# Four score tiles without the split, a first selection round by head, and two splits moved into the gates

## The reference, cut to what matters

```python
def peer_ffn(h, w_q, sub_keys, expert_u, expert_v):      # heads 8, keys 128, top 16
    def block(hb):
        q = (hb @ w_q).reshape(n, PEER_HEADS, 2, PEER_HALF_2)
        s = jnp.einsum('nhcd,hckd->nhck', q, sub_keys).astype(jnp.float32)
        sc, ix = lax.top_k(s, PEER_TOPK)
        cand = sc[:, :, 0, :, None] + sc[:, :, 1, None, :]
        cidx = ix[:, :, 0, :, None] * PEER_N_KEYS + ix[:, :, 1, None, :]
        top, pos = lax.top_k(cand.reshape(n, PEER_HEADS, PEER_TOPK * PEER_TOPK), PEER_TOPK)
        eidx = jnp.take_along_axis(cidx.reshape(n, PEER_HEADS, -1), pos, axis=-1)
        gate = jax.nn.softmax(top, axis=-1)
        act = jax.nn.gelu(jnp.einsum('nhed,nd->nhe', expert_u[eidx], hb), approximate=False)
        return jnp.einsum('nhe,nhed->nd', (gate * act).astype(hb.dtype), expert_v[eidx])
```

## Time and profile before

| what | value |
|---|---|
| median of three runs | 3543.71 us |
| profiled execution, its span | 3543.48 us, 3541.7 us |
| TensorE matmul busy | 3328.0 us, 94% |
| VectorE busy | 2326.8 us, 66% |
| ScalarE busy | 1489.2 us, 42% |
| GpSimd busy | 388.7 us, 11% |
| mean granted TensorE clock | 0.967 |
| load of a tile of `u`, issue to landing, median | 4.2 us |

### The profile page before, as it was taken

How to read it: one execution, slowest core, us unless ns; L and a number is a source line. 1 busy time by engine, 2 the same in 40 slices (tenths; PEclk the granted TensorE clock), 3 DMA queues, 4 the chain that set the end, 5 groups by cost and what they waited for, 6 DMA issues and landing times. The chain is left out here.

```text
span 3541.7 us, 58730 instructions
## 1 busy us (share of the span) xinstructions
PE 3328.0 (94%) x20974; PEld 2901.7 (82%) x20974; DVE 2326.8 (66%) x4418; ACT 1489.2 (42%) x2295; POOL 388.7 (11%) x412
## 2 busy tenths in 40 slices
PE   6889999999988898999999997989788999999998
PEld 5788899999977587899999986578478889999996
DVE  4697666666656588666666665555459766666665
ACT  3336444444445325544444433333333644444444
POOL 0156000000000047200000000000015600000000
PEclk9999999999999699999999998999999999999999
DMA  5420555555544231355555544100242055555553
GB/s 209 154 73 27 187 185 189 189 183 185 189 164 154 84 114 43 125 189 184 185 188 189 184 164 175 63 1 1 95 155 72 31 190 183 185 189 189 184 184 145
DMA packets 127132, 511.72 MB, mean 144 GB/s; under 512 B 14625, under 2 KB 15521, under 8 KB 119713
## 3 DMA queue, kind: packets, MB, share of 16 engines
q1 hardware_dynamic: 127008, 510.09, 40.3%
HBM read 508.99 MB, written 1.05 MB: 144 GB/s over the span
## 5 line engine op out<-in xcount | busy, mean ns | idle before, releaser
L610 PE MATMUL ps<-xh,uhigh 128*128 128x256 f32 x3072 | 870.6, 283 | 0.0
L612 PE MATMUL ps<-xh,ulow 128*128 128x256 f32 x3072 | 869.3, 283 | 0.0
L611 PE MATMUL ps<-xl,uhigh 128*128 128x256 f32 x3072 | 869.2, 283 | 0.0
L610 PEld LDWEIGHTS ps<-xh,uhigh 128*128 128x128 f32 x3072 | 588.3, 192 | 15.0 <-issue 1.4
L611 PEld LDWEIGHTS ps<-xl,uhigh 128*128 128x128 f32 x3072 | 588.3, 192 | 14.3 <-issue 1.4
L612 PEld LDWEIGHTS ps<-xh,ulow 128*128 128x128 f32 x3072 | 588.3, 192 | 0.0
L760 ACT CAST uhigh<-stream 128x1024 fp32r<-128x1024 f32 x336 | 352.8, 1050 | 439.0 <-DMA stream<-in_u 439.0
L992 DVE TENSOR_TENSOR ulow<-stream,uhigh 128x1024 fp32r<-128x1024 f32 x330 | 404.4, 1225 | 192.1 <-ACT uhigh L760 192.1
L997 DVE TENSOR_TENSOR stream<-stream,big 128x256 f32<-128x256 f32 x336 | 218.0, 649 | 413.9 <-ACT stream L822 413.9
L628 PE MATMUL ps<-vhigh,chigh 128*128 128x512 f32 x1536 | 479.7, 394 | 1.5 <-DVE vlow L1008 1.5
L628 PE MATMUL ps<-vlow,chigh 128*128 128x512 f32 x1536 | 475.9, 391 | 0.0
(11 more groups left out here) (502 smaller groups left out, 4387.1 us busy)
## 6 DMA issues: line engine op xcount, KB each, us to landing
stream<-in_u SPq DMA_DIRECT2D x369, 512.0 KB, 4.2
stream<-in_v SPq DMA_DIRECT2D x369, 512.0 KB, 3.5
big<-in_wq SPq DMA_DIRECT2D x24, 1152.0 KB, 7.0
stream<-in_ab_w_in SPq DMA_DIRECT2D x4, 2048.0 KB, 10.9
stream<-in_c_w_qf SPq DMA_DIRECT2D x16, 512.0 KB, 3.5
stream<-in_c_w_ig SPq DMA_DIRECT2D x4, 2048.0 KB, 7.9
big<-in_w_gates SPq DMA_DIRECT2D x4, 2048.0 KB, 7.9
spare<-in_u SPq DMA_DIRECT2D x15, 512.0 KB, 3.7
```

What stands on the lines that cost most here:

```text
L610: pe.matmul(out, high[:, cols], c.xh[:, k, :], start=k == 0, stop=False)
L611: pe.matmul(out, high[:, cols], c.xl[:, k, :], start=False, stop=False)
L612: ins = pe.matmul(out, low[:, cols], c.xh[:, k, :], start=False, stop=k == KD - 1)
```

## The change

Five edits, all in `peer`:

1. The tiles 12 to 15 (`WHOLE` = 12) are no longer split. TensorE multiplies `u` by `xt` as they are, in 8 matmuls for a tile (`whole_scores`), each of which becomes two passes on the engine, as the queries do. Tile 15 comes after the transposes. Banks 2 and 3 hold the results of tiles 14 and 15. No B table may be written before tile 15 is done, so VectorE and GpSimd wait for it.
2. ScalarE's exponentials come before the gelus of tiles 12 to 15, not behind all gelus.
3. The splits of tiles 16 and 17 move into the gates: their rounding before ScalarE's copies 9 and 17, and their subtraction from GpSimd to VectorE, before the weighted rows of quads 20 and 28.
4. The first selection round goes head by head (`halves_by_head`): all of `halves` for a head, then for the other.
5. Two tiles, not four, are scored after the second round of heads, and four after the third.

```diff
-    AFTER = {1: range(0, 4), 2: range(4, 6)}
+    AFTER = {1: range(0, 2), 2: range(2, 6)}
+    WHOLE = 12
...
     def early_bank(n):
-        return c.ps[:, 6 + n % 2, 0:T]
+        return c.ps[:, (6 if n < HELD - 2 else 2) + n % 2, 0:T]
...
             def early(n):
-                sp.wait_ge(low_done, n - 2)
+                if n - 3 < WHOLE:
+                    sp.wait_ge(low_done, n - 2)
+                else:
+                    sp.wait_ge(early_used, n - 2)
...
-            for b in range(2):
-                sp.wait_ge(low_done, HELD - 2 * b)
+            for b in (1, 0):
+                sp.wait_ge(early_used, HELD - 2 * b)
...
+            def whole_scores(n):
+                pe.wait_ge(early_landed[n % 3], 16 * (n // 3))
+                pe.wait_ge(early_gelu, n - 1)
+                for k in range(KD):
+                    ins = pe.matmul(early_bank(n), early_u[n % 3][:, k * P:(k + 1) * P], c.xt[:, k, :],
+                                    start=k == 0, stop=k == KD - 1)
+                ins.then_inc(early_used, 1)
...
-            for n in range(6, HELD):
+            for n in range(6, WHOLE):
                 early_scores(n)
+            for n in range(WHOLE, HELD - 1):
+                whole_scores(n)
...
-            pe.wait_ge(keys_ready, 1)
-            pe.wait_ge(early_gelu, HELD)
-            distances_of(0)
...
+                if x == 0:
+                    pe.wait_ge(early_gelu, HELD - 2)
+                    distances_of(0)
+            whole_scores(HELD - 1)
+            pe.wait_ge(early_gelu, HELD)
...
             act.activation(c.sel[:, 2], c.sel[:, 2], ACT.Exp).then_inc(exp_ready, 1)
+            for n in range(WHOLE, HELD):
+                early_act(n)
...
             for g in range(QUADS):
+                if g in (9, 17):
+                    u_high(0, g // 16, False)
...
+            def halves_by_head():
+
+                for g in range(GROUP):
+                    own = [(tt * GROUP + g) * 2 + half for tt in range(NT) for half in range(2)]
+                    dve.wait_ge(sc_ready, g + 1)
+                    dve.sem_inc(passed, 1)
+                    for q in own:
+                        link.mark(dve.max(TOP[:, q, 0:8], SCq[:, q, :]))
...
-                halves(r)
                 if r:
+                    halves(r)
                     store(r - 1)
+                else:
+                    halves_by_head()
...
-            dve.wait_ge(early_gelu, HELD)
...
+            weighted_rows(0)
+            dve.wait_ge(early_gelu, HELD)
+            plain_rows(0)
...
+                if g in (20, 28):
+                    b = (g - 20) // 8
+                    dve.wait_ge(uh_ready, b + 1)
+                    dve.tensor_tensor(ul[:, b], u[:, b], uh[:, b].bitcast(F32), ALU.subtract).then_inc(u_split, 1)
+                weighted_rows(g)
...
-            for n in range(9, HELD + 2):
+            for n in range(9, WHOLE):
                 early_low(n)
             alone(selt_ready, 1)
+            alone(early_used, HELD)
```

More of the change, by code:

```diff
@@ L757, in u_high @@
                 else:
-                    act.wait_ge(early_used, HELD - 2 * b)
-                    act.wait_ge(low_done, HELD - 2 * b)
+                    act.wait_ge(early_used, WHOLE)
                 act.copy(uh[:, b], u[:, b]).then_inc(uh_ready, 1)
@@ L840, in _ @@
             link = Link(dve, chain)
+            def halves_by_head():
[5 more added lines that the diff above has]
+                        link.mark(dve.max(TOP[:, q, 0:8], SCq[:, q, :]))
+                    link.join_alone(passed)
+                    for q in own:
+                        link.mark(dve.max_index(IDX[:, q, 0:8], TOP[:, q, 0:8], SCq[:, q, :]))
+                        link.mark(dve.match_replace(REST[:, q, :], TOP[:, q, 0:8], SCq[:, q, :], LOWEST))
+                    link.join_alone(passed)
+                    for q in own:
+                        link.mark(dve.max(TOP[:, q, 8:16], REST[:, q, :]))
+                    link.join_alone(passed)
+                    for q in own:
+                        link.mark(dve.max_index(IDX[:, q, 8:16], TOP[:, q, 8:16], REST[:, q, :]))
+                dve.sem_inc(sc_used, 1)
             def halves(r):
@@ L958, in gate_held, with plain_rows @@
                                   ALU.mult).then_inc(dve_moved, 1)
-            for g in range(0, QUADS, 2):
-                if g >= 4:
-                    dve.wait_ge(g_ready, g - 2)
+            def plain_rows(g):
                 for x in (g, g + 1):
@@ L975, in _ @@
                                              bc(c.selt[:, 2, t:t + 4], 2, P), ALU.is_equal, ALU.mult).then_inc(a_ready, 1)
+            weighted_rows(0)
+            dve.wait_ge(early_gelu, HELD)
+            plain_rows(0)
+            for g in range(2, QUADS, 2):
+                if g >= 4:
+                    dve.wait_ge(g_ready, g - 2)
+                plain_rows(g)
+                if g >= 4:
+                    gate_held(g - 4)
+                    gate_held(g - 3)
+                if g in (20, 28):
[3 more added lines that the diff above has]
+                weighted_rows(g)
             for g in range(QUADS - 4, QUADS):
@@ L1021, in early_low @@
             def early_low(n):
-                if n < HELD:
-                    alone(high_done, n + 1)
-                    high, low, raw, done = early_uh[n % 3], early_ul[n % 3], early_u[n % 3], low_done
-                else:
-                    alone(uh_ready, 2)
-                    high, low, raw, done = uh[:, n - HELD], ul[:, n - HELD], u[:, n - HELD], u_split
-                pool.tensor_tensor(low, raw, high.bitcast(F32), ALU.subtract).then_inc(done, 1)
+                alone(high_done, n + 1)
+                pool.tensor_tensor(early_ul[n % 3], early_u[n % 3], early_uh[n % 3].bitcast(F32), ALU.subtract
+                                   ).then_inc(low_done, 1)
             def pick(r):
```

10 lines of the change are left out of this document (2 added, 8 removed).

## The result

| | before | after |
|---|---|---|
| median of the runs, us | 3544.22 (4 runs, 3543.57 to 3545.14) | 3524.47 (4 runs, 3520.92 to 3524.60) |
| profiled execution: time, span, us | 3543.48, 3541.7 | 3524.60, 3522.8 |
| granted TensorE clock over the span | 0.967 | 0.973 |
| copy of quad 3, us from a layer's start, three layers | 132.86, 134.78, 133.34 | 125.22, 125.25, 125.54 |
| copy of quad 3 to the first rounding of `v`, us, three layers | 77.72, 77.71, 77.70 | 79.35, 79.35, 79.35 |

The ratio is 0.9943, with a 95% interval of 0.9931 to 0.9955: 19.8 us faster, against 15.5 forecast (3528.0, range 3516 to 3540). A layer's start is the cast of the activations on ScalarE (L784, before L772); it stands at 130.84, 1227.64 and 2595.76 us after, at 129.40, 1232.10 and 2606.96 before.

What follows compares the result with a forecast made beforehand. VectorE's serial list, stalled by GpSimd's subtractions, was taken to bound the time ahead of the gates, a chain through four engines the gates. 3543.48 - 23.0 (copy of quad 3 earlier) + 7.5 (splits in the gates) = 3528.0 us, range 3516 to 3540.

Steps and rivals of the forecast that it cites:

- The stalls were GpSimd's: Last selection round, cast of keys, product of weights: GpSimd's subtractions hold VectorE; the product ends 8.6, 9.4, 8.6 us earlier.
- the rival in which the long instructions are VectorE's own: Rival, chance 0.04: these VectorE instructions are long whatever GpSimd does, 24.8 us are not won, 3552.8 us, slower.
- Tile 15: Undivided tile between the transposes and the first B tables, 245.4 to 248.9; takes back 4.1 of the first layer's 8.6 us.
- distances and transposes 2.0: TensorE's work just ahead of tile 15, taken as 2.0 us, from at most 2.8 us at 0.78 of the clock.
- about 126 us behind a layer's start in all three layers: Expected place of quad 3's copy in the profile after; its gains were counted as 7.0, 9.0 and 7.0 us.
- The first round by head, two tiles later: nothing: Selection rounds: VectorE's 4.1 us only become waiting for GpSimd's picking; later tiles, zero to 1 us a layer; both counted zero.
- the rival in which round 0 pays: Rival, chance 0.07: the picking and last round come earlier with VectorE, 4.1 us a layer more won, 3515.7 us.
- The splits in the gates: Two ScalarE roundings and two VectorE subtractions in the gates cost 2.5 us a layer, 7.5 in all; bounds nothing to 5.9.
- The idle shares of a mean pair of quads: In the gates, mean idle time, VectorE 0.61 us, ScalarE 0.41; only what a split's instructions exceed it by was counted.
- The rival in which the gates take all back: Rival, chance 0.09: every moved split costs its upper bound, 17.7 rather than 7.5 us in all, 3538.2, no change.
- The port rule: Two-input VectorE and SBUF-reading GpSimd instructions exclude each other; for the gates' subtractions 1.3 us a layer more, 3531.9 us.

## Why the prediction was right, point by point

*The stalls were GpSimd's.* Right. The three small instructions gave back 5.40 us where 5.41 were counted, the cast 1.76 of 1.76, the product 1.41 of 1.42. The product ends 8.7, 9.4 and 8.7 us earlier from the layer's start, for 8.6, 9.4 and 8.6. The subtractions put back brought the stalls back, and only for the instructions that they stood beside. That rules out the rival in which the long instructions are VectorE's own. One reading was loose: the prediction set the ends of L890, L904, L915 and L945 against the rule for two inputs, but L890 (a cast) and L915 (by a scalar) have one. That one-input instructions of this kind are held as well is shown by the fills, which held L945 and L948 of the kernel after.

*Tile 15.* The mechanism was right, the term "distances and transposes 2.0" mis-sized: they took 1.23 us. The prediction named the cause, TensorE busy up to them and at full clock, but priced it from "at most 2.8 us at 0.78 of the clock". That 0.78 is the mean of a window that holds both levels. The narrower window of the kernel before shows the level that the distances and transposes ran at:

```profile
250.00:254.00 4.00, 2.53 (x8) 1.08 (x8) 3.45 (x7) 1.03 (x4) 3.16 (x3) 0.50 0.00 0
```

They took 2.53 us at 0.50, and half of that is 1.27, an estimate that would have been close to the 1.23 measured. Copy 3 so gains 7.64 + 9.53 + 7.79 = 24.96 us rather than 23.0. A small slip adds to this: an event "about 126 us behind a layer's start in all three layers" would gain 7.5 us in the third layer by the prediction's own figures (133.3 - 125.8), and 7.0 were counted. The experiment with the four subtractions shows what the full clock is worth: 2.7 us in the first layer.

*The first round by head, two tiles later: nothing.* Right, both by their own experiment, and for the reason given: L908 behind the picking, and the last round's L917 behind the low part of tile 11. That also excludes the rival in which round 0 pays.

*The splits in the gates.* Right in kind, 7.5 us counted and 3 x 1.64 = 4.9 measured. The copies after fall back by 0.42 us between quads 9 and 12, by 1.0 at quads 20 and 21 and by 0.2 at 28 and 29. The idle shares of a mean pair of quads were too coarse a measure: of two equal subtractions one cost five times the other. The rival in which the gates take all back, 5.9 a layer, is excluded.

The port rule had been weighed for the same subtraction. What the trace shows of VectorE's subtraction, and of GpSimd's B tables around it (count, shortest, middle and longest in ns):

```profile
276.46 1.22 DVE L1024 TENSOR_TENSOR ulow<-stream,uhigh 128x1024 fp32r<-128x1024 f32 x1
```

```profile
L1103 POOL TENSOR_SCALAR stream<-consts,stream x7: 596/598/1357, 273.9 to 278.7; 128x128 f32<-128x128 f32 x7
```

One of seven takes 1357 ns where the middle one takes 598: GpSimd was held for 0.76 us by the subtraction, which itself took its usual 1.22. So the lock was there. But it was no part of the 1.2 us that could be avoided: with the splits at other quads six of GpSimd's instructions are still held, for 1.32 us each, and the gates are 1.2 us a layer shorter. Whether the 0.44 us a layer that are left there (78.15 - 77.71) owe anything to it is not shown. The 3531.9 that the prediction worked out for it, with 1.3 us a layer on top, did not come.

*The sum.* 3543.5 - 25.0 + 4.9 = 3523.4, for 3524.6 of the profiled execution. The 1.2 us between are the unchanged stretches: the first layer starts 1.4 us later, 1.3 are lost between the layers, and 1.6 won behind the last. What moves these was not tried; the kernel before itself ran from 3540.1 to 3546.5 us over the sessions. Two terms were off by 2.0 and 2.6 us in the same direction, and the time came out 3.5 below the forecast; the 1.2 us of the unchanged stretches, which the prediction did not count, hide the rest of their 4.6.

What stays open: why the granted clock fell in the second layer alone in two of the experiments, and again at the program's end in one of them; 0.8 of the 3.2 us behind the last layer with an eighth of tile 15; and how the gain parts between the undivided tiles and the exponentials.

## What to carry to other kernels

A small VectorE instruction that ends with a GpSimd instruction is a stall that can be removed by taking work off GpSimd, and its price is read by subtracting the same instruction's time with GpSimd at rest. Work given to TensorE where it would have been idle cost nothing here up to the moment at which its input was ready, and it brought the serial steps behind it the full clock; beyond that moment each further microsecond was lost. A clock of 0.78 over a window can be 1.00 in one part and 0.50 in the other, so the clock that a step ran at is read from a window around that step alone. An edit that shortens the middle of a chain is worth nothing while a fixed event (here a picking, and one last subtraction) stands behind it, and two equal insertions into a pattern can differ fivefold by their place.

## What the runs showed of the hardware

- A GpSimd fill, which reads nothing, stretched VectorE's one-input TENSOR_SCALAR and CAST over 64 elements from 0.19 and 0.20 to 0.96 to 1.06 us; it left a two-input instruction alone (0.18 us inside a fill of 0.95), and MAX8 too (0.68). A GpSimd subtraction stretched a two-input one (0.18 to 1.88).
- After 4.29 us of idle time TensorE's granted clock stood at 0.70 over the next 9 us, and 16 passes took 5.33 us for 3.62. After 2.1 and 2.54 us of idle time in the second layer it stood at 0.50 over 3 us, and at 0.75 and 0.68; in the first and third layers of the same kernels at 1.00.
- The distances and transposes ahead of the first quad took 2.53 us at a granted clock of 0.50 and 1.23 at 1.00.
- An eighth of a tile rather than a whole one returned 2.4 of the 3.0 us that it freed on TensorE, and 0.5 in the layer in which the clock fell.
